# Output projection of a hybrid decoder step in column pieces of 256, 256 and 512, two of them for all tiles first, with the eighth tile's norm on GpSimd and ScalarE

## Chip, cores and metric

One core of a Trainium2 chip runs the whole kernel. The metric is the device time of one execution in microseconds; the kernel before takes 1090.51 us, the median of three runs.

## What is computed

One layer for 1024 prompt tokens with 16 meta tokens ahead of them, and 8 x 4 sample tokens: T = 1072 rows, in nine tiles of 128 rows (the ninth, LAST, has 48). D is 1024.

```
u,q,k,v = RMSNorm(x) W_in
x  = x + W_out [ pool_mixer(u) ; stickbreak_attn(q,k,v) ]
n  = RMSNorm(x)
x  = x + HierMoE(n)      # 4 groups x 8 experts, top group, top 2 experts in it,
                         # silu(n Wgate[e]) * (n Wup[e]) Wdown[e], D_EXPERT = 512
```

## The kernel before

The kernel is written by hand, engine by engine, with semaphores. Four stages follow each other: projections, attention with pooling, the output projection with the second norm and the router, and the experts.

**Output projection.** `cat` holds the concatenated inputs of the nine tiles, split in a high and a low f32r part; W_out is split likewise. `wsteps` is the list of (column piece n, tile t) that TensorE works off. The pieces are `OCOLS`: 0:256, 256:768 and 768:1024. Piece 0 is done for all tiles first; then each tile has its pieces 1 and 2 in turn. A step of a full tile is 24 matmuls (8 slices of the contraction, three products each), one of tile LAST 16 matmuls. VectorE adds each result to the residual tile `xmid[:, t]` (lines 2112, 2113) and counts in `s_xm`. Once a tile has all its columns, TensorE transposes it (`transpose_mid`, line 2671), ScalarE copies the transpose (`copy_turned`), TensorE makes 36 router logits of it (`logits`, line 2660), ScalarE squares and takes the root (`square_mid`, `root_mid`), and VectorE multiplies the row by gain and reciprocal root into `xg` (`norm_scale`, line 2079) and scales the logits (`scale_logits`, line 2092). SyncE stores the residual to `y_all` (line 1064) and the normed rows to `n_scr` in DRAM (line 1079). Tile LAST has its own way: VectorE multiplies by the gain in three pieces (`gain_last`, line 2059), ScalarE by the reciprocal root (line 1636), and ScalarE's queue stores it (line 1638).

**Router.** The tiles fall in three batches, `BATCHES = [(0,3), (3,6), (6,9)]`. For a batch VectorE picks group and experts (`mark`), makes the gates (`shift`, `exps` on ScalarE, `sum_gates`, `name_gates`) and the one-hot rows of the slots (`name_rows`, `place_slots`); TensorE counts ranks (`ranks`) and builds the tables of row numbers and gates for 32 experts x 96 slots (`tables`, `last_tables`, lines 2704 and 2716). The row numbers end in `tab` (line 2142), by which GpSimd gathers the rows of block 0 from `n_scr` (line 1238), after all stores to `n_scr` have landed. The gates follow in `gtab` (line 2148). Between these TensorE has matmuls on `ident` without a use (`keep_warm`, line 2736).

**Experts.** One block of 96 slots for each of 32 experts: `gate_up_product` (line 2794), silu, `down_product` (lines 2811 to 2819), scatter with add to `y_all`. Each expert's weights are 6 MiB, loaded in 6 halves of 1 MiB by SyncE (line 1036) to a ring of 22 places (`at_half`: ten parts of two halves, `at_ring`, and two halves more) that lies over `cat`, the split W_out, `xmid` and others. So a place can be loaded only when what lies there is dead: a half of a `cat` part when its tile has had all its products, one of `at_xm` when the tiles of `xmid` there are stored, turned and normed. SyncE issues in this order (lines 1066 to 1103): per tile the residual, a half, the normed rows; then what waits for the end of the projection; then, for the rest of the run, each half when the block 22 halves back has been used (`load_behind`).

```
for t in range(LAST):
    store_residual(t)
    sp.wait_ge(s_wo, tile_done(t))
    load_part((0, 1, 3, 4)[t // 2], (t % 2,))
```

Of the kernel before, what the change touches and what calls it, by code (L numbers as in the profile page):

```python
# [23 lines left out]
P = 128  # L24
# [69 lines left out]
def hybrid_step(nc, x_prompt, x_sample, cache_k, cache_v, state_pool, page_table, meta_tokens,  # L94
# [145 lines left out]
    OCOLS = [(0, CG), (CG, 2 * CG), (3 * CG, CG)]  # L240
    NO = len(OCOLS)
    at_o = [at_m + 512, at_e, at_m + 512 + w_part]
# [15 lines left out]
    at_ring = [at_cat[0], at_cat[1], at_xm[0], at_cat[2], at_cat[3], at_xm[1]] + at_wo[0:2] + [at_xm[2], at_wo[2]]  # L258
# [45 lines left out]
    def table(at, limit, shapes):  # L304
# [11 lines left out]
        ("tmp32", [P, NB, NE], F32), ("ek", [P, 2, NB, NE], F32), ("le", [P, NB, EPG], F32)))  # L316

# [3 lines left out]
    def slot_tables(q):  # L321

        lo, n = BATCHES[q][0], BATCHES[q][1] - BATCHES[q][0]
        if q < 2:
            return row_oh[:, :, 0:n, :], rhs[:, :, 0:n, :]
        at = lo - BATCHES[2][0]
        return late_oh[:, :, at:at + n, :], late_rhs[:, :, at:at + n, :]

# [17 lines left out]
    cmp_, = table(at_tmp, at_yo_end, (("cmp", [P, NE, OVMAX], F32),))  # L346
# [304 lines left out]
    wsteps = [(0, t) for t in tiles] + [(n, t) for t in range(NT) for n in (1, 2)]  # L651
    obank = [0, 1, 2, 3, 4, 5, 0, 1, 2, 3] + [s % 3 for s in range(9, len(wsteps) - 1)]
# [7 lines left out]
    def tile_done(t):  # L660

        return wsteps.index((NO - 1, t)) + 1

    def out_ps(s):
        return bank[:, obank[s], 0:OCOLS[wsteps[s][0]][1]]

# [10 lines left out]
    def last_norm_ps(part):  # L677

        free = bank[:, obank[wsteps.index((NO - 2, LAST))], 0:2 * P].rearrange("p (c n) -> p c n", n=P)
# [165 lines left out]
    with nc.allow_non_contiguous_dma(reason="small vectors and broadcasts"), blk as block:  # L845

        @block.sync
        def _(sp):
# [159 lines left out]
            load_w_out(1)  # L1008
            for t in tiles:
# [10 lines left out]
                if t == tiles[1]:  # L1020
                    sp.wait_ge(s_avs, SQ * NPG * NSG)
                    load_w_out(2)
# [44 lines left out]
            load_half(j, expert_of[b], b, b % 2, half)  # L1067
            for t in range(LAST):
# [3 lines left out]
                load_part((0, 1, 3, 4)[t // 2], (t % 2,))  # L1072
                if t == 5:
# [45 lines left out]
        def _(pool):  # L1119
# [90 lines left out]

            chain.link(pool.memset(ones[:, :], 1.0))
# [41 lines left out]
            def moved(b):  # L1253
# [3 lines left out]
                pool.wait_ge(s_sc, scatters(b))  # L1257

# [45 lines left out]
        def _(act):  # L1304
# [318 lines left out]
            for t in range(LAST):  # L1623
# [6 lines left out]
                if t == 7:  # L1630
                    exps(1)
            def scale_last_rows():

                r = ROWS[LAST]
                act.wait_ge(s_lrg, 2)
                act.activation(xg[0][0:r, :], xg[0][0:r, :], ACT.Copy, scale=rs[0:r, 0:1]).then_inc(s_n2, 1)
# [4 lines left out]
            act.activation(hr[:, 0, 0:1], one_col[:, :], ACT.Sqrt)  # L1641
# [3 lines left out]
            scale_last_rows()  # L1645
            exps(2)
# [65 lines left out]
        def _(dve):  # L1712
# [260 lines left out]
            def mark(q):  # L1973
# [16 lines left out]
                for k in range(2):  # L1990
                    chain.done(dve.tensor_tensor(ek[:, k, 0:n, :].rearrange("p t (g e) -> p t g e", g=NGRP),
                                                 by_expert(oh[:, k, ts, :]), by_group(group), ALU.mult))
                chain.settle()
                dve.tensor_tensor(eb[:, ts, :], ek[:, 0, 0:n, :], ek[:, 1, 0:n, :], ALU.add).then_inc(s_eb, 1)
# [30 lines left out]
            def name_gates(q):  # L2025
# [8 lines left out]
                return dve.tensor_tensor(slot_tables(q)[1][:, :, :, NE:2 * NE], ek[:, :, 0:n, :], each(gt[:, :, ts], NE), ALU.mult)  # L2034

            def name_rows(q):
# [4 lines left out]
                chain.done(dve.tensor_tensor(slot_tables(q)[1][:, :, :, 0:NE], ek[:, :, 0:n, :], rows, ALU.mult))  # L2041

            def place_slots(q):
# [5 lines left out]
                chain.link(dve.tensor_tensor(prod[:, :, 0:n, :], ek[:, :, 0:n, :], ranks, ALU.mult))  # L2049
# [5 lines left out]

# [858 lines left out]
```

## Time and profile before

| | us |
|---|---|
| runs | 1089.88, 1090.51, 1091.22 |
| the profiled execution | 1090.2 |
| its span | 1088.4 |
| TensorE busy | 1062.3 (98%) |
| VectorE busy | 399.5 (37%) |
| ScalarE busy | 324.1 (30%) |
| GpSimd busy | 173.5 (16%) |
| output projection, first to last matmul | 409 to 531 |
| first expert product | 549.5 |
| last expert's products start | 1058.4 |

The span runs from the first instruction of the profile to the last; 1.8 us of the execution lie outside it. TensorE is granted its full clock (1.00) in every stretch up to 1050 us. From about 522 us the 16 DMA engines are nearly always busy, too.

### The profile page before, as it was taken

Reading aid. Unit: us, or ns where it says so; the run is one execution under the profiler, and the core shown is the slowest. Engines: PE = TensorE matmul, PEld = TensorE weight load, DVE = VectorE, ACT = ScalarE, POOL = GpSimd, SP = SyncE. Lnnn points to the kernel's source line nnn. Section 1 sums busy time; section 2 is a strip of 40 time slices with the busy share of each in tenths; the row PEclk is TensorE's granted clock in tenths of the full one; section 3 lists DMA queues with packets and bytes.
Section 4 is the critical chain, followed back from the end, with each engine's and each line's share of the span. In section 5 each row is a group of like instructions: output and inputs, shape, how many; then the busy total and the mean of one; then the engine's idle time right before and its main releaser. Section 6 shows DMA issues by size and latency. Waiting matters only on the chain.

```text
span 1088.4 us, 29460 instructions
## 1 busy us (share of the span) xinstructions
PE 1062.3 (98%) x13014; PEld 799.9 (73%) x13014; DVE 399.5 (37%) x723; ACT 324.1 (30%) x619; POOL 173.5 (16%) x159
## 2 busy tenths in 40 slices
PE   8999999999999999999999999999999999999996
PEld 7999999966666549899866666666666666666655
DVE  6336664378875543344722112112112111111121
ACT  6423332166775552222311111111111111111111
POOL 1001200699200000100011111111111111111111
PEclk9999999999999999999999999999999999999998
DMA  7356784000117467767899999999999999999993
GB/s 252 111 161 210 224 271 147 1 13 2 40 35 214 141 232 257 240 226 274 311 368 403 387 385 383 391 385 382 388 377 391 377 388 387 384 388 390 380 383 96
DMA packets 85816, 293.21 MB, mean 269 GB/s; under 512 B 13425, under 2 KB 44849, under 8 KB 60069
## 3 DMA queue, kind: packets, MB, share of 16 engines
q1 hardware_dynamic: 78277, 273.30, 67.2%
q0 software_dynamic: 7280, 17.58, 6.8%
q8 instruction: 105, 1.72, 0.6%
q10 hardware_dynamic: 128, 0.39, 0.1%
q14 instruction: 26, 0.21, 0.1%
HBM read 272.98 MB, written 42.87 MB: 290 GB/s over the span
## 4 chain that ended last, share of the span: by engine, by line
PE 87%; DMA 5%; DVE 4%; ACT 1%; SPq 1%; issue 1%; POOL 0%; DVEq 0%; POOLq 0%; ACTq 0%
PE bank L2794 28%; PE bank L2342 12%; PE bank L2579 8%; PE bank L2811 5%; PE bank L2815 5%; PE bank L2385 4%; PE bank L2819 4%; PE bank L2551 3%; DMA w_all<-in_w_up 3%; PE bank L2514 3%; PE bank L2423 3%; PE bank L2767 2%; DVE keep L1868 1%; SPq L1036 1%; PE bank L2660 1%; PE bank L2446 1%
## 5 line engine op out<-in xcount | busy, mean ns | idle before, releaser
L2794 PE MATMUL bank<-w_all,xeT 128*32 128x256 f32 x6144 | 338.4, 379 | 2.6 <-DMA w_all<-in_w_up 2.3
L2794 PEld LDWEIGHTS bank<-w_all,xeT 128*32 128x32 f32 x6144 | 229.2, 110 | 105.4 <-issue 4.3
L2811 PE MATMUL bank<-w_all,hT 128*32 128x256 f32 x744 | 166.4, 380 | 0.0
L2187 DVE TENSOR_TENSOR hid<-sgl,bank 128x384 f32<-128x384 f32 x32 | 27.5, 860 | 294.3 <-ACT sgl L1661 294.3
L2815 PE MATMUL bank<-w_all,hT 128*32 128x512 f32 x744 | 129.1, 595 | 0.0
L1868 DVE TENSOR_TENSOR_SCAN keep<-keep,unseen 128x1024 f32<-128x1024 f32 (+7 forms) x64 | 94.9, 1516 | 37.8 <-ACT keep L1428 37.7
L2342 PE MATMUL bank<-w_hi,xh 128*128 128x256 f32 x376 | 108.1, 287 | 0.0
L2342 PE MATMUL bank<-w_hi,xl 128*128 128x256 f32 x376 | 105.5, 281 | 0.0
L2342 PE MATMUL bank<-w_lo,xh 128*128 128x256 f32 x376 | 105.5, 280 | 0.0
L2811 PEld LDWEIGHTS bank<-w_all,hT 128*32 128x32 f32 x744 | 79.4, 110 | 26.3
L1661 ACT ACTIVATE sgl<-bank 128x384 f32<-128x384 f32 x32 | 15.7, 491 | 277.7 <-PE bank L2794 277.7
L2579 PE MATMUL bank<-wo_hi,cat 128*128 128x256 f32 (+1 forms) x384 | 89.0, 321 | 0.4 <-issue 0.4
L1238 POOL DMA_INDIRECT xg<-n_scr,tab x32 | 31.6, 989 | 346.7 <-issue 231.5
L1248 POOL DMA_INDIRECT out_y_all<-yo,tab x31 | 44.4, 1433 | 208.2 <-ACT yo L1672 208.2
L2819 PE MATMUL bank<-w_all,hT 128*32 128x256 f32 x744 | 75.5, 379 | 0.0
L2342 PEld LDWEIGHTS bank<-w_hi,xh 128*128 128x128 f32 x376 | 70.8, 188 | 0.8 <-DVE xl L1728 0.4
L2342 PEld LDWEIGHTS bank<-w_hi,xl 128*128 128x128 f32 x376 | 71.1, 189 | 0.0
L2342 PEld LDWEIGHTS bank<-w_lo,xh 128*128 128x128 f32 x376 | 70.8, 188 | 0.0
L2579 PEld LDWEIGHTS bank<-wo_hi,cat 128*128 128x128 f32 x384 | 64.2, 189 | 5.7 <-issue 0.7
L1670 ACT ACTIVATE yo<-bank,gtab 96x512 f32<-96x512 f32 x31 | 21.2, 685 | 152.1 <-PE bank L2811 152.1
L2206 DVE TENSOR_SCALAR yo<-bank,gtab 96x256 f32<-96x256 f32 x31 | 14.9, 480 | 132.2 <-PE bank L2811 132.2
L2579 PE MATMUL bank<-wo_lo,cat 128*128 128x256 f32 (+1 forms) x192 | 61.0, 318 | 0.0
(300 smaller groups left out, 1502.6 us busy)
## 6 DMA issues: line engine op xcount, KB each, us to landing
w_all<-in_w_down SPq DMA_DIRECT2D x64, 1024.0 KB, 30.5
w_all<-in_w_gate SPq DMA_DIRECT2D x64, 1024.0 KB, 26.8
w_all<-in_w_up SPq DMA_DIRECT2D x64, 1024.0 KB, 29.7
k_scr<-in_cache_k SPq DMA_DIRECT2D x32, 256.0 KB, 3.4
v_scr<-in_cache_v SPq DMA_DIRECT2D x32, 256.0 KB, 3.4
pgk<-k_scr SPq DMA_DIRECT2D x32, 256.0 KB, 4.0
w_raw<-in_w_in SPq DMA_DIRECT2D x7, 1024.0 KB, 7.0
pgv<-v_scr SPq DMA_DIRECT2D x4, 1024.0 KB, 6.1
```

Of the source, the lines that this page charges most:

```text
L1248: pool.indirect_dma_start(out=y_all, out_offset=bass.IndirectOffsetOnAxis(ap=rows_named(b, sidx), axis=0), in_=yo[b % 2][:, :], in_offset= ...
L1868: dve.tensor_tensor_scan(back, back, unseen[:, NK - w:NK][:, ::-1], 1.0, ALU.mult, ALU.max).then_inc(s_p, 1)
L2342: last = pe.matmul(proj_ps(s)[0:r, :], a[:, k, row0(t):row0(t) + r], b[n % 2][:, k, :], start=(k == 0 and j == 0), stop=(k == KT - 1 and j ...
L2385: last = pe.matmul(wide_ps(s)[:, 0:cols], a[n % 2][:, k, c:c + P], b[:, k, lo:lo + cols], start=(k == 0 and j == 0), stop=(k == KT - 1 and ...
L2423: last = pe.matmul(z_ps(a)[:, lo:lo + n], qT[rows, hp, row0(t):row0(t) + P], kT[rows, hp, lo:lo + n], start=True, stop=True)
L2514: last = pe.transpose(t_ps(n)[0:keys, k, :], keep_of(u, a)[:, P * i:P * i + keys], ident[:, :])
L2551: last = pe.matmul(o_ps(t)[rows, p, 0:n], v, x, start=(c == 0 and (u != TAIL or p == 0)), stop=(c == ch[-1][0]), skip_group_check=True)
L2579: last = pe.matmul(out_ps(s)[0:r, :], cat_tile(a, t)[:, k, 0:r], b[n][:, k, :], start=(k == 0 and j == 0), stop=(k == KT - 1 and j == 2))
L2794: lasts = [pe.matmul(pair_ps(i)[rows_of(q), g, :, :], xeT[i][:, k, rows_of(g)], pair_of(b, i, k, q), start=(k == 0 and g != 1), stop=(k == ...
L2811: return pe.matmul(y_right_ps(g), hT[:, ft, rows_of(g)], w[ft // 2][:, ft % 2, DA:D], start=first and g != 1, stop=ends, skip_group_check= ...
L2815: pe.matmul(y_left_ps[rows_of(g), :], hT[:, ft, rows_of(g)], w[ft // 2][:, ft % 2, 0:512], start=first, stop=ends, skip_group_check=True)
L2819: lasts = [pe.matmul(y_mid_ps[rows_of(g), :], hT[:, ft, rows_of(g)], w[ft // 2][:, ft % 2, 512:DA], start=first, stop=ends, skip_group_che ...
```

## The change

- `OCOLS` becomes 0:256, 256:512, 512:1024. Pieces 0 and 1 are done for all nine tiles, then piece 2 tile by tile. Tile LAST has four steps of 256 columns.
- The transposes of tile t-1 stand between the two halves of piece 2's contraction of tile t, its logits behind.
- The ring begins with the place of W_out's second split piece (`at_wo[0]`), which is loaded whole once pieces 0 and 1 are done; the other parts move back by one. SyncE's order follows.
- GpSimd multiplies tiles 7 and 8 by the gain (`gain_rows`), in two halves each, and ScalarE scales them (`scale_rows`); VectorE's `gain_last` goes, and its `norm_scale` for tile 7.
- The gates of batch 1 (`sum_gates(1)`, `name_gates(1)`, `exps(1)`, and the gate columns of `tables(1)`) move behind `tab`.
- `keep_warm` calls: 14, 4, 4, 14 become 12, 4, 4, 9.

```
-    OCOLS = [(0, CG), (CG, 2 * CG), (3 * CG, CG)]
+    OCOLS = [(0, CG), (CG, CG), (2 * CG, 2 * CG)]
-    at_ring = [at_cat[0], at_cat[1], at_xm[0], at_cat[2], at_cat[3], at_xm[1]] + at_wo[0:2] + [at_xm[2], at_wo[2]]
+    at_ring = [at_wo[0], at_cat[0], at_cat[1], at_xm[0], at_cat[2], at_cat[3], at_xm[1], at_wo[1], at_wo[2], at_xm[2]]
-    wsteps = [(0, t) for t in tiles] + [(n, t) for t in range(NT) for n in (1, 2)]
-    obank = [0, 1, 2, 3, 4, 5, 0, 1, 2, 3] + [s % 3 for s in range(9, len(wsteps) - 1)]
+    wsteps = [(n, t) for n in range(NO - 1) for t in tiles] + [(NO - 1, t) for t in range(NT)] + [(NO, LAST)]
+    obank = [s % 6 if s < 2 * NT else s % 3 for s in range(len(wsteps))]
...
@@ SyncE
+            sp.wait_ge(s_wo, 2 * NT)
+            load_part(0)
             for t in range(LAST):
                 store_residual(t)
                 sp.wait_ge(s_wo, tile_done(t))
-                load_part((0, 1, 3, 4)[t // 2], (t % 2,))
+                load_part((1, 2, 4, 5)[t // 2], (t % 2,))
...
-                    load_part(5, (0,))
+                    load_part(6, (0,))
...
-                        load_part(2)
+                        load_part(3)
                     else:
-                        load_part(5, (1,))
-            sp.wait_ge(s_wo, len(wsteps) - 1)
-            for q in (6, 7):
+                        load_part(6, (1,))
+            sp.wait_ge(s_wo, len(wsteps))
+            for q in (7, 8):
                 load_part(q)
-            sp.wait_ge(s_wo, len(wsteps))
-            load_part(9, (0,))
             sp.wait_ge(s_yl, 16)
             sp.wait_ge(s_lgp, NT)
             sp.wait_ge(s_ln, 2)
-            load_part(9, (1,))
-            load_part(8)
+            load_part(9)
             sp.wait_ge(s_gn, 2)
+            sp.wait_ge(s_tbp, 4)
@@ GpSimd, ahead of the waits for the stores to n_scr
+            def gain_rows(t, ps):
+                r = ROWS[t]
+                return pool.tensor_tensor(xg[t % 2][0:r, :].rearrange("r (k p) -> r p k", p=P)[:, ps, :],
+                                          xmid[0:r, t, :].rearrange("r (p k) -> r p k", p=P)[:, ps, :],
+                                          gffn[0:r, :].rearrange("r (p k) -> r p k", p=P)[:, ps, :], ALU.mult)
+            pool.wait_ge(s_xm, tile_done(LAST - 1))
+            pool.wait_ge(s_nst[1], 16 * ((LAST - 1) // 2))
+            gain_rows(LAST - 1, slice(0, P // 2))
+            pool.wait_ge(s_lrg, 1)
+            gain_rows(LAST - 1, slice(P // 2, P)).then_inc(s_lrg, 1)
+            pool.wait_ge(s_nst[0], 16 * (LAST // 2))
+            gain_rows(LAST, slice(0, P // 2))
+            pool.wait_ge(s_xm, tile_done(LAST))
+            pool.wait_ge(s_lrg, 2)
+            gain_rows(LAST, slice(P // 2, P)).then_inc(s_lrg, 1)
@@ ScalarE
-                if t == 7:
-                    exps(1)
+            def scale_rows(t):
+                r, i = ROWS[t], t % 2
+                act.wait_ge(s_lrg, 2 if t < LAST else 4)
+                act.activation(xg[i][0:r, :], xg[i][0:r, :], ACT.Copy, scale=rs[0:r, i:i + 1]).then_inc(s_n2, 1)
             copy_turned(LAST - 1)
-            act.activation(hr[:, 0, 0:1], one_col[:, :], ACT.Sqrt)
+            scale_rows(LAST - 1)
             square_mid(LAST)
             root_mid(LAST)
             act.dma_start(y_all[row0(LAST):T, :], xmid[0:ROWS[LAST], LAST, :]).then_inc(s_yl, 16)
-            scale_last_rows()
-            exps(2)
+            scale_rows(LAST)
+            store_last_rows()
+            for q in (1, 2):
+                exps(q)
@@ VectorE
-                if t == LAST:
+                if t >= LAST - 1:
+                    if t == LAST:
+                        dve.wait_ge(s_lrg, 3)
                     dve.reciprocal(rs[0:r, c], rs[0:r, c]).then_inc(s_lrg, 1)
-                    dve.wait_ge(s_lrg, 2)
+                    dve.wait_ge(s_lrg, 1 if t < LAST else 4)
                     return
...
-            sum_gates(2)
+            sum_gates(1)
             dve.wait_ge(s_tbp, 3)
             dve.tensor_scalar(tab[:, 0:NE], tab_ps[:, 0:NE], float(T), None, ALU.add).then_inc(s_ix, 1)
+            chain.link(name_gates(1))
+            sum_gates(2)
             name_gates(2).then_inc(s_gn, 1)
@@ TensorE
             for s in range(2, len(wsteps) - 2):
-                out_product(s)
                 n, t = wsteps[s]
-                if n == 1 and t >= 1:
-                    transpose_mid(t - 1)
...
+                if n < NO - 1 or t == 0:
+                    out_product(s)
+                    continue
+                out_product(s, range(KT)[LEFT])
+                transpose_mid(t - 1)
+                out_product(s, range(KT)[RIGHT])
+                logits(t - 1)
...
-            tables(1)
-            keep_warm(14)
+            tables(1, slice(0, NE)).then_inc(s_tbp, 1)
+            keep_warm(12)
             ranks(2)
             keep_warm(4)
             last_tables(slice(0, NE))
             counts()
             keep_warm(4)
             pe.wait_ge(s_gn, 1)
+            tables(1, slice(NE, 2 * NE))
             last_tables(slice(NE, 2 * NE))
-            keep_warm(14)
+            keep_warm(9)
```

## Rows read from the trace of the kernel before

**Rows 1.** The page: mean busy share of the DMA engines, 40 slices of 27.2 us.
```profile
DMA  7356784000117467767899999999999999999993
```

**Rows 2.** Busy time by stretch; the last columns are TensorE's clock, DMA share, GB/s.
```profile
522.00:531.00 9.00, 8.81 (x60) 7.55 (x60) 7.49 (x19) 4.44 (x8) 0.00 (x0) 1.00 1.00 349
531.00:532.00 1.00, 0.80 (x9) 0.52 (x7) 0.95 (x3) 0.00 (x0) 0.00 (x0) 1.00 0.67 213
...
546.00:547.00 1.00, 1.00 (x12) 1.00 (x11) 0.00 (x0) 0.00 (x0) 0.29 (x2) 1.00 0.66 168
...
555.00:600.00 45.00, 45.00 (x764) 28.88 (x767) 10.62 (x21) 7.48 (x13) 4.92 (x4) 1.00 1.02 395
```

**Rows 3.** The chain that ended last, experts: start, duration, what.
```profile
577.50 10.36 PE bank L2794 x192
...
1006.16 5.28 PE bank L2794 x96
...
1024.08 34.16 DMA w_all<-in_w_up
```

**Rows 4.** Timeline of TensorE at the end: start, duration, idle before and releaser.
```profile
1045.71 5.39 PE L2794 MATMUL bank<-w_all,xeT 128*32 128x256 f32 x96 [0.96 <-DMA w_all<-in_w_up]
```

**Rows 5.** Timeline of SyncE's queue around the end of the projection.
```profile
521.27 0.43 SPq L1036 DMA_DIRECT2D w_all<-in_w_down  x1
...
525.12 0.38 SPq L1036 DMA_DIRECT2D w_all<-in_w_gate  x1
529.44 0.81 SPq L1036 DMA_DIRECT2D w_all<-in_w_up  x2
530.29 1.14 SPq L1036 DMA_DIRECT2D w_all<-in_w_down  x2
531.47 15.23 SPq L1036 DMA_DIRECT2D w_all<-in_w_up  x2
546.74 0.91 SPq L1036 DMA_DIRECT2D w_all<-in_w_gate  x2
547.69 0.67 SPq L1036 DMA_DIRECT2D w_all<-in_w_down  x1
```

**Rows 6.** The chain that ended last, one tile's period in the output projection.
```profile
460.93 2.88 PE bank L2579 x24
...
465.51 5.57 PE bank L2579 x24
471.95 2.88 PE bank L2579 x24
```

**Rows 7.** Timeline of VectorE, from the last tile's gain to the gates.
```profile
532.98 1.05 DVE L2059 TENSOR_TENSOR xg<-xmid,gffn 48x512 f32<-48x512 f32 x1
...
534.12 0.24 DVE L2092 TENSOR_SCALAR lg<-bank,rs 48x36 f32<-48x36 f32 x1
...
542.09 0.19 DVE L2142 TENSOR_SCALAR tab<-bank 96x32 int32<-96x32 f32 x1 [0.20 <-PE bank L2716]
542.20 0.16 DVE L2030 TENSOR_SCALAR gt<-gt 128x3 f32<-128x3 f32 x1
```

**Rows 8.** Timeline of TensorE, gate tables to the first gathered rows.
```profile
543.58 1.24 PE L2716 MATMUL bank<-late_rhs,late_oh 128*96 128x32 f32 x12
544.75 3.39 PE L2736 MATMUL bank<-ident 128*128 128x128 f32 x28
548.33 0.88 PE L2767 MATMUL bank<-ident,xg 96*128 96x96 f32 x8 [0.18 <-DMA xg<-n_scr,tab]
```

**Rows 9.** The chain that ended last: store of the last rows, first gather.
```profile
535.30 7.17 DMA n_scr<-xg
...
543.40 4.88 DMA xg<-n_scr,tab
```

**Rows 10.** Groups of GpSimd by form: shapes, count, busy us, mean ns, idle before.
```profile
L1146 POOL TENSOR_TENSOR vv<-vv,v_up 128x512 f32<-128x512 f32 x8 | 10.6, 1319 | 119.4 <-DMA v_up<-out_v_all 119.4
...
L1181 POOL TENSOR_TENSOR wsmall<-wsmall 128x96 f32<-128x96 f32 x2 | 4.4, 2205 | 0.0
```

More of the change, by code:

```diff
@@ L660, in tile_done, with out_cols @@
     def tile_done(t):
[L662 removed]
+        return wsteps.index((NO if t == LAST else NO - 1, t)) + 1
+    def out_cols(s):
+        n, t = wsteps[s]
+        return (CG * n, CG) if t == LAST else OCOLS[n]
     def out_ps(s):
[L665 removed]
+        return bank[:, obank[s], 0:out_cols(s)[1]]
     def bank_free(s):
@@ L677, in last_norm_ps @@
     def last_norm_ps(part):
-        free = bank[:, obank[wsteps.index((NO - 2, LAST))], 0:2 * P].rearrange("p (c n) -> p c n", n=P)
+        free = bank[:, obank[wsteps.index((NO - 1, LAST))], 0:2 * P].rearrange("p (c n) -> p c n", n=P)
         return free if part else norm_ps(LAST)[:, TURNS[0], :]
@@ L1021, in _ @@
                     sp.wait_ge(s_avs, SQ * NPG * NSG)
+                    load_w_out(1)
+                if t == tiles[3]:
                     load_w_out(2)
@@ L1990, in mark @@
                 for k in range(2):
-                    chain.done(dve.tensor_tensor(ek[:, k, 0:n, :].rearrange("p t (g e) -> p t g e", g=NGRP),
+                    chain.done(dve.tensor_tensor(chosen(q)[:, k, 0:n, :].rearrange("p t (g e) -> p t g e", g=NGRP),
                                                  by_expert(oh[:, k, ts, :]), by_group(group), ALU.mult))
                 chain.settle()
-                dve.tensor_tensor(eb[:, ts, :], ek[:, 0, 0:n, :], ek[:, 1, 0:n, :], ALU.add).then_inc(s_eb, 1)
+                dve.tensor_tensor(eb[:, ts, :], chosen(q)[:, 0, 0:n, :], chosen(q)[:, 1, 0:n, :], ALU.add).then_inc(s_eb, 1)
                 dve.wait_ge(s_eb, 2 * q + 1)
@@ L2040, in name_rows @@
                 rows = tok[:, ts].rearrange("p (x t y) -> p x t y", x=1, y=1).to_broadcast([P, 2, n, NE])
-                chain.done(dve.tensor_tensor(slot_tables(q)[1][:, :, :, 0:NE], ek[:, :, 0:n, :], rows, ALU.mult))
+                chain.done(dve.tensor_tensor(slot_tables(q)[1][:, :, :, 0:NE], chosen(q)[:, :, 0:n, :], rows, ALU.mult))
             def place_slots(q):
@@ L2117, in _ @@
                             turn_copied(part)
-                        dve.wait_ge(s_xm, tile_done(LAST))
-                        gain_last(slice(P // 2, P)).then_inc(s_lrg, 1)
                     norm_scale(t)
@@ L2129, in _ @@
                             dve.wait_ge(s_tbp, 1)
-                        sum_gates(q)
-                        chain.done(name_gates(q))
+                        else:
+                            sum_gates(q)
+                            chain.done(name_gates(q))
                         name_rows(q)
@@ L2695, in counts, with tables @@
                 pe.matmul(count_ps, ones[0:ROWS[-1], :], eb[0:ROWS[-1], LAST, :], start=False, stop=True).then_inc(s_rkp, 1)
-            def tables(q):
+            def tables(q, cols=slice(0, 2 * NE)):
                 lo, hi = BATCHES[q]
@@ L2703, in tables @@
                     for k in range(2):
-                        last = pe.matmul(tab_ps, one_hot[:, k, t - lo, :], named[:, k, t - lo, :],
+                        last = pe.matmul(tab_ps[:, cols], one_hot[:, k, t - lo, :], named[:, k, t - lo, cols],
                                          start=(t == 0 and k == 0), stop=False, skip_group_check=True)
-                last.then_inc(s_tbp, 1)
+                return last
             def last_tables(cols):
@@ L2720, in _ @@
             for s in range(2, len(wsteps) - 2):
-                out_product(s)
                 n, t = wsteps[s]
-                if n == 1 and t >= 1:
-                    transpose_mid(t - 1)
-                if n == NO - 1 and t >= 1:
-                    logits(t - 1)
-                    if t == 5:
-                        ranks(0)
-                    if t == 6:
-                        tables(0)
-                    if t == 7:
-                        ranks(1)
+                if n < NO - 1 or t == 0:
[5 more added lines that the diff above has]
+                logits(t - 1)
+                if t == 5:
+                    ranks(0)
+                if t == 6:
+                    tables(0).then_inc(s_tbp, 1)
+                if t == 7:
+                    ranks(1)
             def keep_warm(n):
```

51 lines of the change are left out of this document (22 added, 29 removed).

## The prediction

> **What bounds the kernel now.** I read the page's strips first. The DMA strip [rows 1] is at 9 from the twentieth slice on, that is for the last half of the span, so the experts' weights are a candidate for the bound beside TensorE, which is busy there too. Next I took busy time by stretch around the handover from projection to experts [rows 2]: the DMA engines are full from 522 us on, except for about a third of a microsecond at 531 and another at 546, and from 555 us they never rest. Then the chain of what ended last. Blocks of experts follow each other at (1006.16 - 577.50) / 26 = 16.49 us [rows 3], which is TensorE's own pace. From 1006.16 three more periods would put the last block's products at 1055.6; by the chain's last DMA they start at 1024.08 + 34.16 = 1058.2, and they stand at 1058.4 in the timeline. So 2.8 us of TensorE's time at the very end are waits for weights, and one of the waits can be seen [rows 4]. This is a kernel with two bounds that nearly touch: in the expert stage the loads fall behind a little with each block until the cushion of 22 halves is gone, three blocks before the end. Two things can move the end:
>
> - the DMA bound: how many bytes are still to be moved once the DMA engines are full, and whether they run dry after that;
> - TensorE's bound: when block 0 starts (549.5), 2.8 us of play behind the DMA bound.
>
> The gain is the smaller of the two, and what follows the last weights (30 us) stays. What happens in the projection counts only through these two.
>
> **The column pieces.** A full tile's period is 11.02 us now, of which 5.57 are the 512-column step and 2.88 the 256-column one [rows 6]. The change moves nine of the short steps ahead, so the last piece runs at 11.0 - 2.8 = 8.3 us (rounded) per tile, and begins 25 us later. The sum of TensorE's work is the same: tile LAST trades one 512-column step for two of 256, worth about 0.1 us. VectorE's work for a tile (add, norm, logits: some 4 us) and the longest batch work (about 4.6) now meet in 8.3 us; the batches fall on different tiles, and by my count an add comes at worst 1.2 us late, while the transposes that need it come 1.5 us later than that. I put the end of the projection at 531.2 as before: 0, with 0.5 at most on either side.
>
> **The loads.** SyncE's queue shows [rows 5]: the half at 521.27 is the twelfth, ten follow (one at 525.1, five by 531.5, the second of that row and four more only at 546 to 548, after GpSimd's gathers). In the new order the count at 522 us is: one as now, two of part 0 at 460, seven with tiles 0 to 6, two of part 3, one of part 6, thirteen in all, and at 8.3 us a tile the last of them has landed before 522. The others: one with tile 7 at about 524.3, one after its normed rows, four at 531.3, three at 546 to 548. So at 522 the new kernel has 9 halves to move, the old one 11 (its twelfth has only been issued): 2.1 MB less. At 395 GB/s [rows 2] that is 5.3 us. It pays with idle time that the old one has not: 3.0 us until tile 7 is done, and some 1.2 between its half and the next, as the normed rows of tile 7 now come by way of GpSimd and ScalarE at about 529.5 instead of 524.7. The old one's two gaps, together 0.7 to 0.8 [rows 2], are filled, since one half less waits for the gathers. 5.3 - 4.2 + 0.8 = 1.9 us gained at the DMA bound, if the engines then stay full.
>
> **Block 0's start.** Now the row numbers are there at 542.3 [rows 7], the last rows' store lands at 535.30 + 7.17 = 542.5, the gather goes out at 543.40 and lands 4.88 us later, at 548.28 [rows 9]. TensorE has finished its gate tables and 28 idle passes at 544.75 + 3.39 = 548.14 and turns the rows at 548.33 [rows 8]: both arms end together. In the changed kernel:
>
> - VectorE, after the row numbers: the gates of batch 2 took from 542.20 to about 543.4, after which TensorE starts at 543.58 [rows 7, 8]. Now batch 1's five instructions come first, 1.2 us, and with them the sum of batch 2's, 0.4: +1.6.
> - TensorE: gate columns of batch 1, 12 passes like the 12 of 1.24 us [rows 8]: +1.2.
> - Idle passes 28 to 18 at 0.121 us each [rows 8]: -1.2.
>
> Sum: TensorE is free at 548.14 + 1.6 = 549.75, against rows landed at about 548.3. So block 0 starts 1.45 us later by this arm.
>
> **GpSimd's share.** The last half of tile 8's gain is on the path: VectorE takes 1.05 us for it at 532.98 [rows 7], and it stands ahead of the reciprocal and the last logits at 534.12. Now GpSimd can begin at the last add (532.3), ahead of VectorE's place, and VectorE waits for it with the logits, `mark(2)`, the ranks and the tables queued behind; ScalarE waits with the last scaling and the store. GpSimd's price for this pattern is in no row. Nearest from below: 1.3 us for 512 elements side by side [rows 10]. From above: 2.2 us, the 128x96 instruction [rows 10], which shows how long GpSimd may take when it is in VectorE's way. I take 1.8, between them, since this pattern costs VectorE twice what plain rows cost. 532.3 + 1.8 + 0.2 (reciprocal) = 534.3 to 534.4: 0.2 to 0.3 us late; bounds 0 (ScalarE's root is there just before 534 anyway, so a faster gain wins nothing) and 0.7. The Trainium skill (GPSIMD Engine Reference, Engine selection) calls GpSimd about twice as slow as VectorE on two inputs; as an estimate by that page, twice 1.05 us is 2.1 us and 0.5 us late. The first three halves have 8 us for themselves. ScalarE's two table loads for the exponentials of batch 1 go, on no path.
>
> **The sum.** Start 1.45 + 0.3 = 1.75 us later. TensorE's bound: 2.8 - 1.75 = 1.0 us gained. DMA bound: block 0 frees its first places at 555.0 now, then at 556.8, a microsecond more until packets flow. The queue at 547 holds 4.6 MB now (four halves, a gather of 0.4 MB), 11.6 us, to 558.6; in the changed kernel it is empty 1.9 us sooner, at 556.7. So about 1.1 us of new idle time, and 1.9 - 1.1 = 0.8 gained. The smaller is 0.8: 1090.2 - 0.8 = 1089.4 for an execution like the profiled one. The median of the runs lies 0.3 above the profiled execution, so 1089.7.
>
> **Rivals.**
> 1. *The start is not late.* Gates or idle passes turn out shorter, or the gather lands with the old start at 549.5. Then the DMA engines do not run dry and all 1.9 us are kept, with up to 0.9 more where the new order leaves fewer gaps than I counted; beyond 2.8 TensorE's own pace stops it. Time 1087.7 to 1088.6. For it: both arms have been within 0.2 us of each other [rows 8, 9]. Against it: the 1.6 us on VectorE are plain instructions in a chain.
> 2. *GpSimd is too slow* (the other side). Its four halves form a chain from about 524.2. If one takes h, the last ends at 524.2 + 4h once h is above 2.0; every microsecond past 534 delays rows, gates and store alike. The gain is gone at h = 2.7 and the kernel is 2.2 us slower at h = 3.2; at 4 us it is 1095. For it: an instruction of 96 elements took 2.2 us where one of 512 took 1.3 [rows 10], so GpSimd can be held up by VectorE. Against it: VectorE's instructions at this place are short, 0.2 to 0.7 us, and many read PSUM. The Trainium skill (SBUF — State Buffer, SBUF: two separate sides) says that GpSimd and a two-input VectorE instruction exclude each other on a shared pair of ports for a whole instruction; the row just named agrees in kind.
> 3. *All is given back.* The DMA engines rest longer than I count at the handover, since the last loads come in one burst behind the stores and the last store of `n_scr` lands 1 to 2 us later for it. Gain 0 to -1.5: 1090.5 to 1092. For it: 7.17 us for a store of 0.2 MB [rows 9] is already mostly queueing.
> 4. *It does nothing that shows*: the earlier megabyte only moves idle time. That lies inside my forecast and rival 3.
>
> **How the numbers follow.** Within 0.2% of 1090.51, about what a measurement of this kernel can tell from no change, is 1088.3 to 1092.7. Forecast 0.5 (1088.7 to 1090.4), rival 1 0.24, rival 2 0.12, rival 3 0.14. Of rival 1 about 0.2 lie below 1088.3; of rival 2 about 0.1 above 1092.7, and two in a hundred are left for a late projection. Faster 0.2, same 0.68, slower 0.12. The range takes in the forecast, rival 3 and most of rival 1, and of rival 2 what a late half of a microsecond makes: 1087.8 to 1092.0.
>
> **What the new profile would show.** The 512-column steps of full tiles 8.3 us apart, the projection's end at 531.2. Loads: 13 halves issued by 522, 9 after, DMA idle near 523 and 529.5 and not at 546. GpSimd's halves at 1.3 to 2.2 us, the last logits scaled at 534.1 to 534.8. The row numbers at 542.3 to 542.9, the gate tables starting at 545.2, block 0 at 551.2. The waits for weights in the last three blocks shrink from 2.8 us to about 1. Wrong would prove me a projection that ends over 1 us off, GpSimd's halves above 2.7 us, block 0 at 549.5 or earlier, or a DMA share below 0.9 anywhere between 560 and 1050.

## The result, and the profile after

The changed kernel takes 1093.06 us (median of 21 runs, 1092.3 to 1096.28), the kernel before 1091.71 us in as many runs beside it (1089.83 to 1093.35): ratio 1.0018, 95% interval 1.0012 to 1.0024. The forecast was 0.8 us less; by the ratio it is 2.0 us more, by the two medians 1.35. 1093.06 lies above the range of 1087.8 to 1092.0. A part of that distance is not the change: the range was built on 1090.51, and the kernel before measured 1.2 us more this time. The ratio applied to 1090.51 gives 1092.5, which is still outside. The profiled execution of the changed kernel took 1095.32 us with a span of 1093.6, against 1088.4 for the span before. That difference is larger than the one of the medians: its clock stood at half for 6.8 us in the first 20 us, and so the projection's first product starts at 411.27 instead of 409.20. Where the two profiles are set side by side I take these 2.07 us off ("shifted"); the ratio comes from the runs.

The page of the changed kernel, TensorE's granted clock and the DMA engines' share in 40 slices of 27.3 us:

```profile
PEclk8999999999999999999989999999999999999999
DMA  7357785000116567489899999999999999999993
```

Beside [rows 1] the DMA strip has hardly changed. The clock's 8 in the twenty-first slice is new. The handover from projection to experts, in windows (after the span: PE, weight loads, VectorE, ScalarE, GpSimd busy, the clock, DMA share, GB/s):

```profile
526.00:527.00 1.00, 1.00 (x10) 1.00 (x10) 0.51 (x1) 0.46 (x1) 0.41 (x1) 1.00 0.00 0
...
544.00:545.00 1.00, 1.00 (x8) 0.96 (x9) 0.86 (x5) 0.00 (x0) 0.02 (x1) 1.00 1.03 434
545.00:546.00 1.00, 0.41 (x4) 0.22 (x2) 0.83 (x6) 0.00 (x0) 1.00 (x1) 0.71 0.99 418
546.00:555.00 9.00, 8.31 (x44) 8.18 (x45) 1.19 (x5) 0.00 (x0) 1.54 (x4) 0.50 1.01 297
555.00:556.00 1.00, 1.00 (x9) 0.86 (x7) 0.00 (x0) 0.31 (x1) 0.00 (x0) 0.67 1.00 418
...
560.00:564.00 4.00, 4.00 (x72) 2.58 (x68) 1.40 (x4) 1.47 (x2) 0.65 (x1) 1.00 0.52 126
```

From 545.4 to 555.6 TensorE had its lower level, 1.2 GHz. The fall comes just as TensorE runs out of work (its last idle pass ends at 544.25 + 1.16 = 545.41), not behind the standstill that follows. Behind that the DMA engines run half dry at 560 to 564, where [rows 2] has them full: block 0 frees its places too late. What TensorE did meanwhile, with its idle time before and the releaser in brackets:

```profile
544.25 1.16 PE L2765 MATMUL bank<-ident 128*128 128x128 f32 x8
546.69 2.13 PE L2731 MATMUL bank<-rhs,row_oh 128*96 128x32 f32 x12 [1.28 <-DVE late_rhs L2068]
548.63 2.24 PE L2743 MATMUL bank<-late_rhs,late_oh 128*96 128x32 f32 x12
550.80 4.21 PE L2765 MATMUL bank<-ident 128*128 128x128 f32 x18
554.80 1.24 PE L2797 MATMUL bank<-ident,xg 96*128 96x96 f32 x8
556.28 4.96 PE L2824 MATMUL bank<-w_all,xeT 128*32 128x256 f32 x88 [0.23 <-issue]
...
1062.43 5.38 PE L2824 MATMUL bank<-w_all,xeT 128*32 128x256 f32 x96
1068.70 5.39 PE L2824 MATMUL bank<-w_all,xeT 128*32 128x256 f32 x96 [0.89 <-DMA w_all<-in_w_gate]
```

An idle pass is one of the two that each call of `keep_warm` makes: 18 passes are 9 calls. Read these against [rows 8]. TensorE stands still for 1.28 us while VectorE names the gates of both batches; then 12 passes that took 1.24 us take 2.13 and 2.24, and 18 idle passes take 4.21 (at 0.121 us each they are 2.2). Block 0 starts 145.0 us behind the projection's first product, before 140.3: 4.7 us late, where 1.75 were forecast. (Block 0 is the first expert's block, the last block that of the last expert.) And the last block's first half starts without a wait for weights, unlike [rows 4]: 1062.43 - 2.07 = 1060.4, which is 1055.6 + 4.7 up to rounding. In this execution the kernel has become bound by TensorE.

What had been foretold of the loads and of VectorE's and GpSimd's work is mostly there. The chain (one tile's 512-column step), SyncE's queue, VectorE and GpSimd of the changed kernel, from four views:

```profile
495.84 2.73 PE bank L2606 x12
...
504.01 2.73 PE bank L2606 x12
```
```profile
533.17 1.41 SPq L1048 DMA_DIRECT2D w_all<-in_w_down  x2
534.62 1.22 SPq L1048 DMA_DIRECT2D w_all<-in_w_gate  x2
547.95 0.80 SPq L1048 DMA_DIRECT2D w_all<-in_w_up  x2
550.95 0.33 SPq L1048 DMA_DIRECT2D w_all<-in_w_down  x1
```
```profile
528.42 1.38 DVE L2075 TENSOR_TENSOR rhs<-ek,tok 128x192 f32<-128x192 f32 x1
...
535.79 0.25 DVE L2121 TENSOR_SCALAR lg<-bank,rs 48x36 f32<-48x36 f32 x1
...
543.76 0.19 DVE L2165 TENSOR_SCALAR tab<-bank 96x32 int32<-96x32 f32 x1 [0.50 <-PE bank L2743]
```
```profile
528.29 2.65 POOL L1226 TENSOR_TENSOR xg<-xmid,gffn 128x512 f32<-128x512 f32 x2 [0.40 <-DVE rs L2100]
534.13 1.28 POOL L1226 TENSOR_TENSOR xg<-xmid,gffn 48x512 f32<-48x512 f32 x1 [3.19 <-DVE xmid L2137]
```

The tiles' period is 8.17 us. The last logits are scaled at 535.79 - 2.07 = 533.7 and the row numbers stand at 541.7, each 0.4 us earlier than [rows 7].

### The profile page after: what moved, and what is told of

Same layout as the page of the kernel before. It is cut to its first block, busy times and chain, and to the rows that moved or that the text cites. A ratio compares the mean times of both kernels' runs of the same rounds, so it can differ in the third digit from the quotient of the medians.

```text
span 1093.6 us, 29493 instructions
## 1 busy us (share of the span) xinstructions
PE 1067.5 (98%) x13028; PEld 805.7 (74%) x13028; DVE 396.9 (36%) x721; ACT 322.1 (29%) x617; POOL 178.4 (16%) x163
## 4 chain that ended last, share of the span: by engine, by line
PE 88%; DVE 4%; DMA 3%; SPq 1%; issue 1%; ACT 1%; POOL 0%; DVEq 0%; POOLq 0%; ACTq 0%
PE bank L2824 28%; PE bank L2367 12%; PE bank L2606 8%; PE bank L2841 5%; PE bank L2845 5%; PE bank L2410 4%; PE bank L2849 4%; PE bank L2576 3%; PE bank L2539 3%; DMA w_all<-in_w_gate 3%; PE bank L2448 3%; PE bank L2797 2%; SPq L1048 1%; DVE keep L1902 1%; PE bank L2687 1%; PE bank L2471 1%
```

## The experiments

My theory after the result, C: the late gates let TensorE stand still, its clock falls, and block 0 starts late by more than the 2.8 us of play. ("Play" is how late block 0 may start before the end moves.) All runs are beside the kernel before on the same chip (its medians there 1091.56, 1091.74 and 1091.65 us). Each was also profiled once; the table at the end holds what those profiles show. Numbers of idle passes, here and in the expectations, are calls of `keep_warm` from now on, each of which is two passes in the rows.

**More idle calls ahead of the gates.** The changed kernel, with

```diff
-            keep_warm(12)
+            keep_warm(14)
             ranks(2)
 ...
-            keep_warm(4)
+            keep_warm(9)
             pe.wait_ge(s_gn, 1)
```

> The changed kernel with 14 idle calls in place of 12 ahead of the last ranks, and 9 in place of 4 ahead of the wait for the gates, so that TensorE has work in the 1.28 us in which it stood still at 545.4. Theory C (the clock): the changed kernel lost its time because TensorE's granted clock fell from 2.4 to 1.2 GHz from 545.8 to 555.7, right behind that standstill, and doubled gate tables, idle passes and transposes. Then here the clock stays at 1.00 there, gate tables take 2.4 us and the last idle passes 2.2, block 0 starts some 141 us behind the projection's first product (145.0 in the changed kernel, 140.3 in the one before), the DMA engines do not run dry at 560, and the time is 1.5 to 2.2 us below the kernel before. Rival P (the path): the start is late by the router's longer chain and the clock matters little: block 0 at 144 or later, the time at or above the kernel before. Rival G (GpSimd in the way): GpSimd's gain halves delay VectorE and with it everything, nothing changes here beyond 0.5 us.

1091.7 us, ratio 1.0002 (0.9992 to 1.0012). Its profile, TensorE and then a window:

```profile
546.42 1.21 PE L2731 MATMUL bank<-rhs,row_oh 128*96 128x32 f32 x12 [0.16 <-DVE late_rhs L2068]
547.46 1.30 PE L2743 MATMUL bank<-late_rhs,late_oh 128*96 128x32 f32 x12
548.69 2.27 PE L2765 MATMUL bank<-ident 128*128 128x128 f32 x18
550.80 0.83 PE L2797 MATMUL bank<-ident,xg 96*128 96x96 f32 x8
551.92 5.39 PE L2824 MATMUL bank<-w_all,xeT 128*32 128x256 f32 x96 [0.30 <-issue]
```
```profile
546.00:555.00 9.00, 8.54 (x113) 7.30 (x115) 1.54 (x4) 0.49 (x1) 2.33 (x4) 1.00 0.96 341
```

The same gates, equally late, but with 0.16 us of standstill and the clock at 1.00 from there to block 0: from the first gate table to block 0 it is 5.5 us instead of 9.6. Seven calls that compute nothing, two ahead of the last ranks and five ahead of the gates, take the loss back. (The two intervals touch, at 1.0012. Which of the seven calls matter was not parted. Nor was the clock full throughout: it stood at half from 535.0 to 538.4, under the idle passes ahead of the last ranks.) The gain that I still expected from the loads does not come, which the later runs are about.

**The deferral alone, in the kernel before.**

```diff
@@ VectorE (not shown: exps(1), sum_gates(1) and name_gates(1) in their new places, a buffer for them)
                         if q == 1:
                             dve.wait_ge(s_tbp, 1)
-                        sum_gates(q)
-                        chain.done(name_gates(q))
+                        else:
+                            sum_gates(q)
+                            chain.done(name_gates(q))
 ...
-            tables(1)
-            keep_warm(14)
+            tables(1, slice(0, NE)).then_inc(s_tbp, 1)
+            keep_warm(12)
 ...
+            tables(1, slice(NE, 2 * NE))
             last_tables(slice(NE, 2 * NE))
-            keep_warm(14)
+            keep_warm(9)
```

> The kernel before with one part of the change alone: gates of batch 1 behind the row numbers, its gate columns a pass of their own, idle calls 12, 4, 4, 9. Theory C: TensorE stands still some 1.4 us ahead of the gate tables, its clock falls to 1.2 GHz, block 0 starts 5 to 6 us later than in the kernel before (some 145.5 behind the first product), the time is 2 to 3.5 us above it. Rival P: the clock stays up, block 0 starts 1.5 us later, and the time is within 0.5 us. Rival G: nothing of the loss is here, as GpSimd has no part in it: equal to the kernel before.

1094.41 us, ratio 1.0026 (1.0014 to 1.0038). Column pieces, ring and GpSimd are as before, so none of them is needed for the loss, which is there whole and with the same picture (only that the clock fell at 543.3 here, 0.9 us ahead of the standstill, and stayed down through it; so this standstill did not bring it down):

```profile
545.12 2.13 PE L2713 MATMUL bank<-rhs,row_oh 128*96 128x32 f32 x12 [0.89 <-DVE late_rhs L2040]
547.05 2.24 PE L2725 MATMUL bank<-late_rhs,late_oh 128*96 128x32 f32 x12
549.23 4.21 PE L2745 MATMUL bank<-ident 128*128 128x128 f32 x18
```

**The deferral alone, filled.** The same with 14 and 9 idle calls in place of 12 and 4.

> The kernel before with the gates of batch 1 named late, as in the run that did this alone (1.0026), and now 14 and 9 idle passes of TensorE instead of 12 and 4 ahead of the wait for the gates. Theory C (the deferral costs time only through TensorE's clock, which falls when the engine stands still ahead of the gate tables): clock 1.0 from 530 to 560, gate tables 1.2 to 1.3 us each instead of 2.1, block 0's first product 141.8 to 142.5 us behind the projection's first product (before 140.3), that is later by less than the 2.8 us that cost nothing: ratio 1.000, within 0.999 to 1.001. Rival V (the deferral on VectorE itself costs the time, clock or not): ratio 1.002 or more again.

1091.94 us, ratio 1.0002 (0.9992 to 1.0011). The interval lies wholly below that of the run before, with the same work on VectorE, so rival V falls (its sign was 1.002 or more): five more idle calls ahead of the gates and two ahead of the ranks take the loss back here as well. The expectation on the profile was wrong: the clock still fell twice for 3.4 us, at 535.5 and 549.2, and block 0 started at 144.2, not at 141.8 to 142.5. The profiled execution (1092.58) is slower than this kernel's median, and one profile does not say how often the clock falls. The mean clock of each execution does, roughly: 0.990 to 0.994 (median 0.992) in the 21 of the changed kernel and 0.989 to 0.993 (0.992) with the gates late alone; 0.990 to 0.996 (0.995) in the run with 14 and 9 calls, 0.992 to 0.998 (0.995) here, and 0.991 to 0.998 in the kernel before beside them.

**The gates back in their old place, in the changed kernel.** `exps(1)` on ScalarE, `sum_gates(1)` and `name_gates(1)` on VectorE, one pass of `tables(1)`, idle calls as before.

> The changed kernel with the gates of batch 1 back in their old place (summed and named at tile 7, their exponentials there, one table pass over all 64 columns, idle calls 14, 4, 4, 14 as before); pieces, ring, and GpSimd's and ScalarE's norm stay. Theory C: no standstill ahead of the gate tables, the clock stays at 1.00, block 0 starts 139.5 to 140.3 us behind the projection's first product, the time is 1.8 to 2.8 us below the kernel before, the 0.8 MB of weights that are moved ahead at 550. Rival P: the same start, as the path is short again, so this run alone does not part C from P; the first one does. Rival D (the earlier loads bring nothing): equal to the kernel before within 0.5 us.

1093.27 us, ratio 1.0018 (1.0006 to 1.003). A miss, with a cause that I had not seen. ScalarE, and one line of VectorE:

```profile
526.86 1.28 ACT L1629 ACT_TABLE_LOAD   x1
528.15 0.21 ACT L1629 ACTIVATE gex<-gex 128x12 f32<-128x12 f32 x1
528.27 0.19 ACT L1631 ACTIVATE gt<-gt 128x3 f32<-128x3 f32 x1
528.37 1.01 ACT L1638 ACTIVATE nT<-bank 128x1024 f32<-128x1024 f32 x1
...
535.69 1.28 ACT L1650 ACT_TABLE_LOAD   x1
```
```profile
528.82 0.17 DVE L2057 TENSOR_REDUCE gw<-gex 128x3 f32<-128x12 f32 x1 [1.50 <-ACT gt L1631]
```

The exponentials' table now loads ahead of the root's for the last tile, and I had left out the early square root that hid the second load. The last logits are scaled at 536.6 (shifted) instead of 533.7: 1.3 us by the second load, and 1.6 us because VectorE waits 1.50 us for the exponentials and adds the last tile's result that much later. The clock was at half here too, from 535.1 to 542.0. So this run says nothing on pieces and loads alone.

**The gates half way.** `exps(1)` and that early root between the eighth tile's norm and the ninth's squares; the sums on VectorE while it waits for the ninth root; 3, 11, 4, 4 and 22 idle calls.

> The changed kernel with the gates of batch 1 named earlier: their exps between the eighth tile's norm and the ninth's squares (ScalarE is free there for 3.3 us), their sums on VectorE while it waits for the ninth tile's root, and their tables in one pass as in the kernel before; 22 idle passes behind the last gate tables. The logits are scaled about 0.3 to 0.5 us later than in the changed kernel, the gate tables end near 545 us, so no standstill of over 0.7 us ahead of them and no fall of the clock there. Theory Q: the gather is issued near 543.5, lands 7 to 8 us later, block 0 at 141.5 to 143 us behind the first product, ratio 0.9995 to 1.0005. Rival E: 0.9975 to 0.999. Rival V (VectorE's extra work on its way to the logits is worse than the late gates): ratio above 1.001.

1092.99 us, ratio 1.0013 (1.0003 to 1.0023): the number is that of rival V, but what the profile shows is the clock. It fell for 6.8 us at 532.9, the 12 passes of `tables(1)` took 2.13 us, the gather went out at 545.74 and block 0 started at 144.0, not at 141.5 to 143.

**Fewer idle calls in the kernel before** (the four ahead of the gates taken out: 14, 4, 0, 14; the first number stays at 14, not 12 as the expectation has it).

> The kernel before with fewer idle calls alone: 12, 4, none, 14 in place of 14, 4, 4, 14; no useful work is moved. Theory C in its plain form (a standstill of about a microsecond ahead of the gate tables brings the clock down): the clock falls to 0.5 behind 543.6, gate tables take 2.3 us and the last idle passes 6.8, block 0 starts 4.4 us later, the time is 1.5 to 2.5 us above. If the 0.9 us here are too short, nothing changes: clock 1.00, block 0 at 140.3, time equal within 0.5 us, and the length of the standstill matters. Rivals P and G: no change.

1091.37 us, ratio 1.0004 (0.9995 to 1.0013). The clock fell to half for 6.8 us at 543.6, behind a standstill of 0.75 us; block 0 started 2.7 us late (4.4 expected), and no cost shows: these are the 2.8 us of play.

**A late start with a full clock**, the kernel before with 34 idle calls instead of 14 behind its gate tables.

> The kernel before with 34 idle passes of TensorE behind its gate tables instead of 14: block 0 starts about 5 us later, with the clock full and all else as before. Theory S (the time grows by the start's delay less 2.8 us of play, whatever brings the delay): 2.0 to 2.4 us more, ratio 1.0018 to 1.0022. Rival K (it is the slow clock under block 0 and not the delay of its start that costs): ratio below 1.001.

1094.92 us, ratio 1.0029 (1.0016 to 1.0041); the clock is 1.00 from 544 to 555. Rival K falls: the delay of block 0 costs at full clock, too. In the profile 4.45 us of delay put the last block 1.5 us later, about the 1.7 beyond the play. But that execution (1092.39) is one of the fastest of the twelve; by the medians the cost is 3.3 us, and where the rest goes was not looked into.

**An earlier start.** As the first run, with 3 idle calls instead of 9 behind the gate tables; then with 4 more between the halves of the last tile's transposes.

> The changed kernel with idle passes 14, 4, 9 ahead of the gate tables as in the run that brought it to 1.0002, and 3 instead of 9 behind them. Its block 0 can start when the gathered rows have landed (issue near 544.7, about 4.9 us): 150.5 to 151.2 instead of 551.9 in that profile's time, counted from its first product 140.8 to 141.4 us instead of 142.05. Theory L (the 0.85 MB by which the loads lead at 550 is lost between 570 and 600 because the ring's halves come free only as TensorE goes through block 0, so a late block 0 takes the lead away): the lead stays above 0.3 MB at 600 and the ratio is 0.998 to 0.9995. Rival E (the lead is lost to something else, or the end is set by bytes and not by it): ratio 1.000 as before, the lead gone by 600 all the same.

> As the run above, and 4 idle passes of TensorE (into a bank that is free then) between the two halves of the last tile's transposes, where it stood still for 0.47 us and its clock then fell to 0.5 for 3.4 us, so that the ranks came 1.1 us late for VectorE. Theory C: no fall of the clock between 530 and 560, the ranks' wait of VectorE back at about 0.6 us, tab and the gather about 1 us earlier than in the run above, block 0 at 140.0 to 140.8 us behind the first product; theory L then has the lead at 600 at 0.6 MB or more and a ratio of 0.9965 to 0.9985. Rival E: ratio 1.000. Rival W (the fall has another cause than this standstill): clock 0.5 again near 534 and a time like the run above.

1093.9 us, ratio 1.001 (0.9998 to 1.0022), and 1093.63 us, ratio 1.0014 (1.0003 to 1.0026). Both miss. TensorE of the first:

```profile
548.08 0.94 PE L2765 MATMUL bank<-ident 128*128 128x128 f32 x6
552.07 1.54 PE L2797 MATMUL bank<-ident,xg 96*128 96x96 f32 x8 [3.05 <-DMA xg<-n_scr,tab]
```

Without the passes TensorE waits 3.05 us for the gathered rows, and its clock falls for 6.8 us, now under block 0. The first gather took 7.9 us in both runs, not the 4.88 of [rows 9]. In the second run the fall near 534 is gone, as theory C had it, but another of 3.4 us comes at 542.9. The loads' lead was gone by 600 in both, theory L's sign of being wrong (1.6 and 1.1 MB behind the kernel before). That gave a new theory, Q: the loads that are ahead hold up the gather.

**Cover for the gather, and loads held back for it.** The second of these kernels with 12 calls at the end; and the same kernel with 3, in which SyncE waits:

```diff
-            for q in (7, 8):
-                load_part(q)
+            load_part(7)
+            sp.wait_ge(s_gl[0], 16)
+            load_part(8)
```

> The changed kernel with idle passes wherever TensorE stood still in the handover: 4 between the halves of the last tile's transposes, 14, 4, 9 ahead of the gate tables, and 12 behind them, so that they cover the gather's landing (7.8 us behind its issue in the two runs before). Block 0 at 142.3 to 143.0 us behind the projection's first product (before 140.3). Theory Q (the loads' lead is what delays the gather: 7.5 to 7.9 us where the loads run through it, 3.8 to 4.9 us where their queue has run out; so the start is late by about what the lead gives, and lies at the edge of the 2.8 us of play): no fall of the clock from 543 to 556, ratio 0.9995 to 1.0005. Rival E (the lead does pay once the clock is full): ratio 0.9975 to 0.999.

> As the run with the earlier start and the 4 passes in the gap, but SyncE issues the two halves of the ninth part (loads of 1 MB each) only when the gathered rows have landed. Theory Q: the gather lands 4 to 5.5 us behind its issue instead of 7.8, the loads pause near 545 to 548 and their lead at 550 falls from 0.8 MB to 0.2 MB or less, block 0 at 139.5 to 141 us; both gains cancel, ratio 0.999 to 1.0005. Rival H (the gather's time is its own and not the loads'): landing 7 us or more again, block 0 where it was, and the lost lead makes the ratio 1.001 or more.

Covered: 1091.31 us, ratio 1.0005 (0.9993 to 1.0017). Held: 1093.81 us, ratio 1.002 (1.0008 to 1.0031). The landing of the gathers for the first two blocks (with the loads held only the second one's is on record) and the DMA windows, covered and then held; the last line is the held load's issue:

```profile
DMA to landing us min/median/max: 6.9/7.1/7.4
```
```profile
544.00:546.00 2.00, 2.00 (x13) 2.00 (x12) 1.06 (x4) 0.00 (x0) 1.67 (x4) 0.50 1.00 422
546.00:548.00 2.00, 2.00 (x22) 1.96 (x21) 0.00 (x0) 0.00 (x0) 0.02 (x1) 0.87 1.09 272
548.00:550.00 2.00, 2.00 (x19) 1.96 (x19) 0.19 (x1) 0.00 (x0) 0.00 (x0) 1.00 0.96 225
```
```profile
DMA to landing us min/median/max: 3.6/3.6/3.6
```
```profile
542.00:544.00 2.00, 2.00 (x16) 1.88 (x17) 1.31 (x8) 0.00 (x0) 0.27 (x1) 1.00 0.09 37
544.00:546.00 2.00, 1.84 (x19) 1.65 (x17) 1.65 (x7) 0.00 (x0) 1.70 (x2) 1.00 0.24 37
546.00:548.00 2.00, 2.00 (x22) 1.92 (x22) 0.11 (x1) 0.00 (x0) 0.60 (x3) 1.00 0.64 199
```
```profile
547.43 0.80 SPq L1048 DMA_DIRECT2D w_all<-in_w_gate  x2
```

With the loads out of its way the gather lands in half the time (the first one was issued at 543.73, and SyncE, which waits for its landing, goes on at 547.43), and block 0 starts at 139.7, earlier than in any other run. This bears out the mechanism of Q. Its sum was wrong: the loads paused for longer than I had set, the lead of 0.6 MB at 550 became a lag of 1.2 MB, TensorE waited 5.8 us for weights, and the kernel is slower by 0.2%. The Trainium skill (DMA: Bandwidth & Descriptors, Queues, rings and completion order) says that each DMA engine takes packets in turn from the queues that have work for it; 3.6 against 6.9 to 7.4 us for the same rows agrees in kind.

What one profile of each kernel shows; all times count from the projection's first product, so without shifts:

| kernel | profiled execution, us | block 0 | last block | waits for weights between | clock at half, 526 to 560 | ratio |
|---|---|---|---|---|---|---|
| before | 1090.2 | 140.3 | 649.2 | 2.3 | 0 | 1 |
| after | 1095.32 | 145.0 | 651.2 | 0 (0.9 in the last) | 10.2 | 1.0018 |
| after, 14 and 9 idle calls | 1090.72 | 142.1 | 649.1 | 0.9 | 3.4 | 1.0002 |
| after, all gaps filled | 1089.8 | 142.9 | 648.8 | 0 | 3.4 | 1.0005 |
| after, loads held | 1095.02 | 139.7 | 652.9 | 5.8 | 0 | 1.002 |
| after, gates back | 1092.73 | 143.8 | 650.4 | 0.5 | 6.8 | 1.0018 |
| after, gates half way | 1091.53 | 144.0 | 650.0 | 0 (0.2 in the last) | 6.8 | 1.0013 |
| after, earlier start | 1095.73 | 144.3 | 654.6 | 1.7 | 3.4 + 6.8 | 1.001 |
| the same, 4 calls more | 1092.17 | 143.3 | 651.2 | 0 | 3.4 + 6.8 | 1.0014 |
| before, gates late | 1093.97 | 145.3 | 651.7 | 0.3 | 10.2 | 1.0026 |
| the same, filled | 1092.58 | 144.2 | 651.3 | 1.0 | 3.4 + 3.4 | 1.0002 |
| before, fewer idle calls | 1090.94 | 143.0 | 649.3 | 0.2 | 6.8 | 1.0004 |
| before, late start | 1092.39 | 144.8 | 650.7 | 0 | 0 | 1.0029 |

The ratios come from all executions of each kernel, the other columns from one; the deferral filled and the late start show that the two need not agree.

Where there is no wait and no slow clock, block 0 to last block is 505.9 us (552.13 to 1058.04 with all gaps filled). That is TensorE's bound, and it gives the last block at 140.3 + 505.9 = 646.2 for the kernel before: 3.0 us of play, my 2.8. (The waits in the table, counted where TensorE's rows show idle time, add up to less: 2.3 of these 3.0 us, and 5.8 of 7.3 with the loads held.)

## Why the prediction was wrong

- **What bounds the kernel.** Right: two bounds that nearly touch, 2.8 us of play. A start 2.7 us late cost nothing that shows, one 4.45 and ones 4.7 and 5.0 us late cost 0.2 to 0.3%. (With the deferral filled the one profile has a start 3.9 us late and the eleven runs show no cost; that profile's clock fell twice, and the other executions may have started earlier.)
- **Column pieces and projection.** Right. Period 8.17 us (forecast 8.3), end 531.0 shifted (531.2).
- **Loads.** The count was right: 13 halves issued by 522, nine after, DMA engines idle at 524 to 527 and not at 546. The gap of 1.2 us forecast near 529.5 is not there: the share is 0.91 to 0.95 from 529 to 532. Counted from the same point of both traces, its queue had moved 1.2 MB more than before at 520, 1.9 MB more at 522 (2.1 forecast) and 0.65 MB more at 550 (0.25 to 0.65 MB in the variants that keep this order and do not hold the loads).
- **Block 0's start: here it failed.** The step "+1.6, +1.2, -1.2" took every duration at TensorE's full clock. VectorE's part was even a little less: the gate tables start at 546.69 - 2.07 = 544.6, forecast 545.2. But with the gates 1.6 us later TensorE runs out of work at 545.41, and from there the clock is at half for 10.2 us: through a standstill of 1.28 us, the 12 passes added, the 12 of batch 2's gates, the 18 idle ones and the turning of the gathered rows. Between gate tables and block 0 lie 9.6 us instead of the 5.5 of the run with more idle passes: 4.1 us from the clock, and 544.6 + 9.6 = 554.2 where I had 551.2. I had priced idle passes as time to be saved; seven calls more of them ahead of this wait brought the ratio from 1.0018 to 1.0002, and from 1.0026 to 1.0002 in the kernel before with late gates. The change has fewer of them where it has more to wait for. That the lower clock is what costs is shown; what brings the clock down is not, since the falls at 545.41 and 543.29 do not follow the standstill that I had named.
- **GpSimd.** Mis-sized: 1.28 to 1.30 us for a half, not 1.8, so the logits came 0.4 us earlier and not 0.2 to 0.3 later. The rival "GpSimd is too slow" had the right sign for another reason, and the run with the gates late alone, GpSimd untouched, excludes it as the cause.
- **The sum.** TensorE's bound: 4.7 - 2.8 = 1.9 us lost, against a forecast of 1.0 gained; measured 0.0018 x 1091.7 = 2.0, or 1.35 by the medians. That one profile and the ratio meet within 0.1 us is in part luck: the profiled execution is the fourth slowest of its 21.
- **Why the kernel does not win with more idle calls either.** The forecast's other half, 0.8 us at the DMA bound, rests on the gather of 4.88 us in [rows 9], which ran while the queued loads ran out. I had counted a third of a microsecond of idle DMA time there, at 546 [rows 2]; the engines' share was 0.86 from 544 to 546 and 0.80 from 546 to 548, some 0.7 us in all. When the loads no longer stop there, the first gathers take 6.9 to 7.9 us in four of the five profiles in which the loads ran on (5.4 to 5.8 in the one with 14 and 9 calls); with the gates half way, where the share sank to 0.30, they took 3.7 to 3.9. So the start is late even where TensorE has done its part: with all gaps filled the rows land at 141.3, before at 139.1, which puts block 0 at 142.5 at the earliest, and it started at 142.9, with 2.6 of the 2.8 us of play gone. In that profile TensorE never waits for weights, and 0.2 to 0.4 us is all that could be won. Rival 3, "all is given back", comes nearest.
- **Open.** In the run with 14 and 9 idle calls block 0 started at 142.1 and 1 us could have been won; yet its lead of 0.6 MB at 570 was gone at 600 (0.1 MB behind). SyncE issued each later load 1.7 to 1.8 us (shifted) after its time in the kernel before, as TensorE frees the places, and a load landed 6 to 8 us behind its issue instead of 9 to 12, so fewer were under way. Why the engines moved less with those, at a share near 1, was not tried. Nor does a standstill explain each fall of the clock: with all gaps filled it still fell for 3.4 us at 543.1, behind 2.7 us with TensorE busy. The kernel with the loads held has the same instructions and the same gaps on TensorE up to that point, and its clock did not fall.

No version here beats the kernel before.

## What to carry to other kernels

Before an edit lets TensorE wait longer, ask at which clock the work behind that wait will run, and price it at both levels; more idle passes ahead of the wait may be all that it needs. A transfer that is quick in the profile of before may be quick only because others have stopped; if the edit fills that pause, price it as shared. And measure the play between two bounds (here a few idle passes more or less) before counting a gain at one of them.

## What the runs showed of the hardware

- The clock stood at half for 10.2 us in the executions with a standstill of 1.28 or 0.89 us at the gates, for 6.8 us with one of 0.75. It fell as the first of these began, 0.9 us ahead of the second and 0.1 us behind the third. Where 0.16 us were left there it stayed full through the gate tables in four profiles, and fell for 3.4 us a little later in one of them. The Trainium skill (TensorE: Matmul & The Clock Gate, Part 1) calls half rate the default, from which activity releases the engine; the trace agrees in the two levels, 0.50 and 1.00.
- While GpSimd multiplied two inputs (528.29 to 530.9), VectorE's two-input instruction of 192 elements took 1.38 us; before it took 0.35.
- A gather of 96 rows landed in 3.6 us beside idle DMA engines and in 5.4 to 7.9 us among weight loads.
